# Layout transposes of a hybrid decoder step moved from TensorE to DMA transposes on SyncE's queue

## The chip, the cores and the metric

The kernel runs on the 8 cores of one Trainium2 chip. Each core works on its own two prompt sequences and its own 16 sample sequences, with no traffic between cores. The metric is the device time of the slowest core in microseconds (us). PE is TensorE, ACT is ScalarE, DVE is VectorE, POOL is GpSimd and SP is SyncE; SP computes nothing and only issues DMAs, in the order of its queue.

## The reference

Two layers over prompt sequences of 2048 + 16 tokens and over 8 new tokens of each sample sequence, width 1024. Cut to what matters:

```python
for l in range(DEPTH):
    q, k, v, u = _project(hp, ln1[l], w_in[l])           # rmsnorm, then 1024 -> 512 | 128 | 128 | 512
    a = _prompt_attention(rope(q), rope(k), v, sinks[l]) # 8 heads of 64, window 128, two key/value heads
    pm = _pool_mix(u, ...)                               # causal pooling over 2/4/8/16 tokens, then a small matmul
    hp = hp + concat([a, pm]) @ w_out[l]                 # 1024 x 1024
    hp = hp + _mlp(hp, ln2[l], w_up[l], w_down[l])       # rmsnorm, 1024 -> 4096, relu squared, 4096 -> 1024
y_prompt = _rmsnorm(hp, ln_f)[:, N_META:]
```

The sample sequences go through the same layers with cached keys and values.

## The kernel before, in words

Tokens are cut into 34 tiles of 128 rows: tile 0 holds the meta tokens, tiles 1 to 32 the two prompt sequences, tile 33 the sample tokens. `MACROS` puts them into groups of at most four tiles, 9 groups in each of the two layers, 18 in all. Each group has two phases. `att_phase(q)` runs `att_tile` for each tile: load `h`, normalise it (`norm_T` with gain 0), project (`inproj`), rotate, transpose q and k, pool, scores, exponentials, probabilities times values (`st_pv`), output projection (`oproj`), and normalise again (`norm_T` with gain 1) into `xn2T`. Two tiles are in flight; they use the two sets of buffers (`xhat`, `xnT`, `P`, `PT`, `a`, `mixT`) in turn. `mlp_phase(q)` streams the two large weight matrices in 8 pieces of 1 MB each through two buffers each and alternates blocks of 8 matmuls: `up` (1024 to 512 columns of one piece, for all tiles of the group at once) and `dn` (back to 1024, tile by tile, added into `h` by DVE).

The attention phase of group q + 1 is written beside the MLP phase of group q, and there are 8 slots for `h`, so a tile of group q + 1 can only be loaded when group q - 1 has left its slot through the MLP and the store.

A matmul contracts over the partitions, so everything that becomes an operand must first be turned. Before the change all of this is done on PE through a bank of PSUM and copied out by ACT or DVE: the normalised rows `xhat` into `xnT` or `xn2T` (8 blocks of 128 by 128), the probabilities `P` into `PT` (8 blocks for each of two head groups, `st_pt`) and the attention output `a` into `mixT` (2 blocks for each head group, `st_at`).

The order on every engine is fixed at build time by `list_schedule`. It walks through all operations with a cost for each, lets attention work (`cls` 0) go ahead of MLP work (`cls` 1) when both are ready, and writes the order down; on the chip every engine then works strictly in that order and waits on semaphores. For a DMA it counts:

```python
DMA_BW = {"pool": 330e3, "sp": 200e3, "act": 200e3}
HOP_LAT = 0.35
            issue_end = st + c
            dma_free[e] = max(issue_end, dma_free[e]) + nb / DMA_BW[e]
            fin = dma_free[e] + 2.0
            eng_free[e] = issue_end
```

Of the kernel before, what the change touches and what calls it, by code (L numbers as in the profile page):

```python
# [309 lines left out]
def build_program():  # L310
# [38 lines left out]
    S = Sched()  # L349
# [18 lines left out]
    xn2T_t, _ = sbn("xn2T", 2, [128, 8, 512], BF16)  # L368
# [31 lines left out]
    mix_t, mix_b = sbn("mixT", 2, [128, 8, 128], BF16)  # L400
    kvf_t, kvf_b = sb("kvf", [128, 256])
    st_t, st_b = sbn("stat", 8, [128, 64])
    st_b2 = [Buf("statb%d" % i) for i in range(8)]
# [14 lines left out]
    banks = Banks((4, 5, 6, 7))  # L418
# [21 lines left out]
    def dma(eng, out, in_, reads=(), writes=(), sembuf=None, after=()):  # L440
        return dmas(eng, [(out, in_)], reads=reads, writes=writes, sembuf=sembuf, after=after)

    def act(fn, reads, writes, pw=(), cost=None):
# [16 lines left out]
    first_pe = []  # L460
# [110 lines left out]
    def norm_T(hs, gi, dstT, dstT_b, par, bank):  # L571
# [8 lines left out]
        dve(lambda e: e.scalar_tensor_tensor(out=xh[:], in0=h_t[hs][:], scalar=sT[:, 2:3], in1=g_t[gi][:], op0=ALU.mult, op1=ALU.mult),  # L580
            [h_b[hs], sB, g_b[gi]], [xhb], cost=1.29)
        trps = ps_t[bank].bitcast(BF16)

# [184 lines left out]
    def att_tile(l, ti, hs, par, q, j):  # L768
# [7 lines left out]
        if l or ti not in preloaded:  # L776
            load_x(l, ti, hs)
        while True:
            bk = banks.take(1)
            if bk:  # L780
                break
            yield False
        norm_T(hs, 0, xnT, xnTb, par, bk[0])
        if l == 0 and ti == 0:
            load_rest()
        banks.give(*bk)
        yield True
# [143 lines left out]
        if kind != "sample":  # L931
# [53 lines left out]

            def st_pt(g, bpt):
                ptps = ps_t[bpt].bitcast(BF16)

                def ptr(e):
                    r = None  # L990
                    for h4 in range(4):
                        for hf in range(2):
                            c = (h4 * 2 + hf) * 128
                            r = e.transpose(out=ptps[:, c:c + 128], in_=P[:, g * 4 + h4, hf * 128:(hf + 1) * 128], identity=ident_t[:])  # L994
                    return r
                pe(ptr, [Pg[g], ident_b], [ps_b[bpt]], cost=0.45)
                dst = PT[:, g * 4:(g + 1) * 4, :, :].rearrange("p h f t -> p (h f t)")
                if g == 0:
                    act(lambda e: e.activation(out=dst, in_=ptps[:, :], func=AF.Copy), [ps_b[bpt]], [PTg[g]], cost=1.05)
                else:  # L1000
                    dve(lambda e: e.tensor_copy(out=dst, in_=ptps[:, :]), [ps_b[bpt]], [PTg[g]], cost=0.69)
# [16 lines left out]

            def st_at(g, baT):
                aTps = ps_t[baT].bitcast(BF16)  # L1020

# [27 lines left out]
            yield True  # L1049
            b, = yield from grab(1)  # L1050
            st_pt(0, b)
            banks.give(b)
            st_exp(1, *s1)
# [5 lines left out]
            banks.give(b)  # L1059
            b, = yield from grab(1)  # L1060
            st_pt(1, b)
            banks.give(b)
            yield True
            b, = yield from grab(1)
            st_at(0, b)
            banks.give(b)
            b, = yield from grab(1)
            st_pv(1, b)
            banks.give(b)
            yield True  # L1070
            b, = yield from grab(1)
            st_at(1, b)
            banks.give(b)
            yield True
# [20 lines left out]
        yield True  # L1095
        while True:
            bk = banks.take(1)
            if bk:
                break
            yield False  # L1100
        norm_T(hs, 1, xn2T_t[q % 2][:, :, j * 128:(j + 1) * 128], xn2T_b[q % 2][j], par, bk[0])
        banks.give(*bk)
        yield True
# [195 lines left out]
```

How the kernel before makes its waits and increments, by code:

```python
    def emit(engname, eng):  # L181
        seen = {}
        for idx in order[engname]:
            o = ops[idx]
            waits = {}
            for d in o.deps:
                od = ops[d]
                if _skip_edge(od, o):
                    continue
                s, v = od.tok
                k = id(s)
                if k not in waits or waits[k][1] < v:
                    waits[k] = (s, v)
            for k, (s, v) in waits.items():
                if seen.get(k, 0) >= v:
                    continue
                eng.wait_ge(s, v)
                seen[k] = v
            r = o.fn(eng)
            if o.dma:
                assert len(r) == o.ndma, (len(r), o.ndma)
                for ins in r:
                    ins.then_inc(o.tok[0], 16)
            elif o.tok is not None:
                r.then_inc(o.tok[0], 1)
        if engname == "sp":
            for s, v in finals:
                eng.wait_ge(s, v)
```

## Time and profile before

| | |
|---|---|
| median of 3 runs | 2930.97 us (2930.91 to 2939.81) |
| the profiled execution, device time | 2944.05 us |
| its span on the slowest core (core 1) | 2942.3 us |
| PE busy | 2779.2 us, 94% of the span |
| DVE busy / ACT busy | 1522.4 us / 1535.3 us, 52% each |
| DMA queues, share of 16 engines | 42.5% (POOL's queue), 9.5% (SP's queue) |
| chain that ended last | PE 87%, DMA 9% |

The span is the time from the first to the last instruction of a core. A share of busy time is a mean over stages; the stage from 2262 to 2424 us is one whole period of the program (four tiles through attention, four through the MLP) and is looked at by itself below.

### The profile page before, as it was taken

To read this page: it belongs to the slowest core of one execution; us is meant where nothing else is said; L and a number is where in the kernel's file an instruction comes from. 1 tells how busy PE (TensorE), PEld (TensorE's weight loads), DVE (VectorE), ACT (ScalarE), POOL (GpSimd) and SP (SyncE) were. 2 spreads that over 40 slices of the span, in tenths; PEclk is the share of its full clock that TensorE was granted. 3 is DMA by queue.
4 is the path that set the end of the run, shared out by engine and by line. 5 is a ranking of instruction groups with operands and counts; after the bars stand their busy time and mean duration, and the time that the engine had idled before them with its cause. 6 is when DMAs were issued, how large, how long until landed. Compare 5 with 4: busy or idle time off the path is not lost.

```text
span 2942.3 us, 52160 instructions; the slowest of 8 cores (2901.3 to 2942.3 us)
## 1 busy us (share of the span) xinstructions
PE 2779.2 (94%) x17074; PEld 1446.1 (49%) x17074; DVE 1522.4 (52%) x3188; ACT 1535.3 (52%) x3835; POOL 195.2 (7%) x336
## 2 busy tenths in 40 slices
PE   4789988979899999999999999999899999999997
PEld 2455434445455555545455555454454545555544
DVE  2444534545355555545555555555455555555543
ACT  3545534545355555545454655555554655555543
POOL 1000100100000000000000000000000000000000
PEclk8999989999999999999999999999999999999999
DMA  9599996664756647353625332443325242342446
GB/s 177 88 145 197 178 243 122 146 169 125 195 137 161 189 113 205 101 195 123 229 87 201 114 142 93 154 132 115 117 99 188 87 167 105 117 158 87 160 145 228
DMA packets 115648, 436.41 MB, mean 148 GB/s; under 512 B 18732, under 2 KB 45324, under 8 KB 80216
## 3 DMA queue, kind: packets, MB, share of 16 engines
q0 software_dynamic: 89024, 335.80, 42.5%
q1 hardware_dynamic: 26360, 97.28, 9.5%
q8 instruction: 143, 2.34, 0.3%
q14 instruction: 121, 0.99, 0.1%
HBM read 442.32 MB, written 79.22 MB: 177 GB/s over the span
## 4 chain that ended last, share of the span: by engine, by line
PE 87%; DMA 9%; ACT 1%; issue 1%; DVE 1%; SPq 0%; POOL 0%; ACTq 0%; DVEq 0%; POOLq 0%
PE ps_all L1165 29%; PE ps_all L1147 29%; PE ps_all L801 10%; PE ps_all L1089 8%; DMA s_wup<-w_up 2%; PE ps_all L587 2%; PE ps_all L952 2%; PE ps_all L994 2%; DMA s_wout<-w_out 2%; DMA h_mid<-s_h 1%; DMA s_wdn<-w_dn 1%; DMA s_h<-x_p 1%; PE ps_all L954 1%; PE ps_all L953 1%; DMA s_kc<-ck 1%
## 5 line engine op out<-in xcount | busy, mean ns | idle before, releaser
L1165 PE MATMUL ps_all<-s_wdn,s_aT 128*128 128x512 bf16 x4288 | 1037.5, 382 | 21.6 <-DMA s_wdn<-w_dn 12.5
L1147 PE MATMUL ps_all<-s_xn2T,s_wup 128*128 128x512 bf16 (+2 forms) x4608 | 1023.8, 367 | 19.5 <-DMA s_wup<-w_up 13.2
L1169 DVE TENSOR_TENSOR s_h<-s_h,ps_all 128x512 f32<-128x512 f32 x1072 | 735.1, 686 | 549.1 <-PE ps_all L1165 524.7
L1147 PEld LDWEIGHTS ps_all<-s_xn2T,s_wup 128*128 128x128 bf16 x4608 | 445.1, 98 | 470.1 <-issue 31.0
L1151 ACT ACTIVATE s_relu<-ps_all 128x512 f32<-128x512 f32 (+2 forms) x576 | 326.0, 566 | 626.1 <-PE ps_all L1147 613.8
L1165 PEld LDWEIGHTS ps_all<-s_wdn,s_aT 128*128 128x128 bf16 x4288 | 406.1, 98 | 450.6 <-issue 36.1
L1152 ACT ACTIVATE s_aT<-s_relu 128x512 bf16<-128x512 f32 (+2 forms) x576 | 346.2, 601 | 39.0 <-PE ps_all L1165 5.4
L801 PE MATMUL ps_all<-s_win,s_xnT 128*128 128x512 bf16 (+1 forms) x1632 | 315.0, 350 | 22.5 <-DMA s_win<-w_in 12.6
L976 ACT ACTIVATE s_P<-ps_all,s_stat 128x256 bf16<-128x256 f32 x520 | 239.2, 476 | 91.4 <-DVE s_stat L966 91.3
L1089 PE MATMUL ps_all<-s_wout,s_mixT 128*128 128x512 bf16 x1072 | 249.8, 384 | 2.0 <-ACT s_mixT L1029 1.9
L801 PEld LDWEIGHTS ps_all<-s_win,s_xnT 128*128 128x128 bf16 x1632 | 160.7, 99 | 176.9 <-issue 36.7
L575 ACT ACTIVATE s_xhat<-s_h 128x1024 bf16<-128x1024 f32 x135 | 142.6, 1056 | 145.7 <-DVE s_h L1092 86.0
L960 DVE TENSOR_REDUCE s_stat<-ps_all 128x2 f32<-128x512 f32 x260 | 167.8, 684 | 86.0 <-PE ps_all L954 84.8
L580 DVE SCALAR_TENSOR_TENSOR s_xhat<-s_h,s_stat,s_gbc 128x1024 bf16<-128x1024 f32 x135 | 172.7, 1280 | 64.5 <-ACT s_stat L579 63.9
L436 POOL DMA_DIRECT2D s_wup<-up_bf x128 | 67.8, 530 | 1860.9 <-PE ps_all L1147 1262.8
L820 DVE TENSOR_TENSOR s_ropet<-ps_all,s_rope 128x160 f32<-128x160 f32 x68 | 22.0, 324 | 297.8 <-ACT s_vu L811 294.5
L1092 DVE TENSOR_TENSOR s_h<-s_h,ps_all 128x512 f32<-128x512 f32 x134 | 92.1, 687 | 150.6 <-PE ps_all L1089 148.7
L1089 PEld LDWEIGHTS ps_all<-s_wout,s_mixT 128*128 128x128 bf16 x1072 | 104.8, 99 | 122.2 <-issue 8.9
L587 PE MATMUL ps_all<-s_ident,s_xhat 128*128 128x128 bf16 x1080 | 85.6, 224 | 48.5 <-DVE s_xhat L580 45.1
L587 PEld LDWEIGHTS ps_all<-s_ident,s_xhat 128*128 128x128 bf16 x1080 | 72.5, 100 | 75.9 <-issue 52.5
L976 ACT ACTIVATION_READ_ACCUMULATOR s_P<-ps_all,s_stat 128x1 f32 x520 | 108.7, 209 | 0.0
L952 PE MATMUL ps_all<-s_masks,s_ident 128*128 128x512 bf16 x260 | 98.5, 379 | 2.2 <-ACT s_qT L882 1.3
(130 smaller groups left out, 2016.3 us busy)
## 6 DMA issues: line engine op xcount, KB each, us to landing
s_wup<-up_bf POOLq DMA_DIRECT2D x128, 1024.0 KB, 6.4
s_wdn<-dn_bf POOLq DMA_DIRECT2D x128, 1024.0 KB, 7.2
h_mid<-s_h SPq DMA_DIRECT2D x34, 512.0 KB, 8.1
s_h<-h_mid SPq DMA_DIRECT2D x34, 512.0 KB, 7.9
s_h<-x_p SPq DMA_DIRECT2D x32, 512.0 KB, 9.3
s_wup<-w_up POOLq DMA_DIRECT2D x16, 1024.0 KB, 18.0
s_wdn<-w_dn POOLq DMA_DIRECT2D x16, 1024.0 KB, 19.2
y_p<-s_h SPq DMA_DIRECT2D x32, 512.0 KB, 5.5
```

Source lines behind the costliest of these rows:

```text
L580: dve(lambda e: e.scalar_tensor_tensor(out=xh[:], in0=h_t[hs][:], scalar=sT[:, 2:3], in1=g_t[gi][:], op0=ALU.mult, op1=ALU.mult), [h_b[hs] ...
L587: r = e.transpose(out=trps[:, k * 128:(k + 1) * 128], in_=xh[:, k * 128:(k + 1) * 128], identity=ident_t[:])
L801: r = e.matmul(ps_t[bank][:, 0:c1 - c0], lhsT=xnT[:, k, :], rhs=win_t[:, k, c0:c1], start=(k == 0), stop=(k == 7))
L952: e.matmul(ps_t[bk][:].rearrange("p (s h k) -> p s h k", s=2, h=2), lhsT=ident_t[:], rhs=mask4d, start=True, stop=False)
L960: dve(lambda e, v4=v4, cc0=cc0: e.tensor_reduce(out=sT[:, cc0:cc0 + 2], in_=v4, axis=AX.XY, op=ALU.max), [ps_b[bk]], [], pw=[Ba], cost=0.69)
L976: act(lambda e, v3=v3, hh=hh: e.activation(out=P[:, hh, :].rearrange("p (s k) -> p s k", s=2), in_=v3, func=AF.Exp, bias=sT[:, 16 + hh:17 ...
L1089: r = e.matmul(ps_t[bo][:], lhsT=mix[:, c, :], rhs=wout_t[:, c, hf * 512:(hf + 1) * 512], start=(c == 0), stop=(c == 7))
L1147: r = e.matmul(ps_t[bk][:, 0:n], lhsT=wup_t[s][:, k, fc * 128:(fc + 1) * 128], rhs=x2[:, k, 0:n], start=(k == 0), stop=(k == 7))
L1151: act(lambda e: e.activation(out=r_t[ri][:, 0:n], in_=ps_t[bk][:, 0:n], func=AF.Relu), [ps_b[bk]], [r_b[ri]], cost=0.18 + n / 1210.0)
L1152: act(lambda e: e.activation(out=aT[:, fc, 0:n], in_=r_t[ri][:, 0:n], func=AF.Square), [r_b[ri]], [], pw=[aTb], cost=0.21 + n / 1210.0)
L1165: r = e.matmul(ps_t[db][:], lhsT=aT[:, fc, j * 128:(j + 1) * 128], rhs=wdn_t[s][:, fc, hf * 512:(hf + 1) * 512], start=(fc == 0), stop=(fc ...
L1169: dve(lambda e, hf=hf, db=db: e.tensor_tensor(out=h_t[hs][:, hf * 512:(hf + 1) * 512], in0=h_t[hs][:, hf * 512:(hf + 1) * 512], in1=ps_t[d ...
```

## The change

From the second group on (`q` above 0) the three kinds of turning are done by a DMA transpose that SP issues, straight from SBUF to SBUF, with no PSUM bank, no PE instruction and no copy. The sample tile keeps its own transposes inside its attention, and q and k are still turned on PE. The first group keeps the old way. For `list_schedule` a DMA transpose costs 0.1 us of issue and twice its bytes at 200,000 bytes per us, plus the 2.0 us of every DMA.

```diff
+    mixT_sem = [[Buf("mixT%d_%d" % (i, g)) for g in range(2)] for i in range(2)]
...
+    def dma_T(out, in_, reads, writes, pw=(), sembuf=None):
+        def fn(e):
+            return [e.dma_start_transpose(out=out, in_=in_)]
+        return S.op("sp", fn, reads=reads, writes=writes, pwrites=pw, dma=1, sembuf=sembuf, cost=0.1, nbytes=2 * _nbytes(in_))
...
+        if bank is None:
+            t_op = dma_T(dstT, xh[:], [xhb], [dstT_b], sembuf=dstT_b)
+            if gi == 0:
+                first_pe.append(t_op)
+            return
...
+        by_pe = q == 0
...
-        norm_T(hs, 0, xnT, xnTb, par, bk[0])
+        norm_T(hs, 0, xnT[:], xnTb, par, bk[0] if by_pe else None)
...
             def st_pt(g, bpt):
+                if bpt is None:
+                    dma_T(PT[:, g * 4:(g + 1) * 4, :, :].rearrange("p h f t -> p (h f) t"), P[:, g * 4:(g + 1) * 4, :].rearrange("p h k -> p (h k)"),
+                          [Pg[g]], [PTg[g]], sembuf=PTg[g])
+                    return
...
             def st_at(g, baT):
+                if baT is None:
+                    dma_T(mix[:, g * 2:g * 2 + 2, :], asb[:, g * 256:(g + 1) * 256], [ag[g]], [], pw=[mixb], sembuf=mixT_sem[par][g])
+                    return
...
-            b, = yield from grab(1)
-            st_pt(0, b)
-            banks.give(b)
+            if by_pe:
+                b, = yield from grab(1)
+                st_pt(0, b)
+                banks.give(b)
+            else:
+                st_pt(0, None)
...
-        norm_T(hs, 1, xn2T_t[q % 2][:, :, j * 128:(j + 1) * 128], xn2T_b[q % 2][j], par, bk[0])
-        banks.give(*bk)
+        norm_T(hs, 1, xn2T_t[q % 2][:, :, j * 128:(j + 1) * 128], xn2T_b[q % 2][j], par, bk[0] if by_pe else None)
+        if by_pe:
+            banks.give(*bk)
```

Counted over the program, SP's queue gets 383 DMA transposes: 66 into `xnT`, 65 into `xn2T` and 126 into `PT`, each of 128 by 1024 bf16 values (256 KB), and 126 into `mixT` of 128 by 256 values (64 KB). It had 200 rows of DMAs before.

Since the costs changed, `list_schedule` also writes another order. On SP, over one late period (four tiles of layer 1), the queue held only stores of finished tiles and loads of new ones:

```order
L436 DMA y_p<-s_h 128x1024
L436 DMA s_h<-h_mid 128x1024
L436 DMA y_p<-s_h 128x1024
L436 DMA s_h<-h_mid 128x1024 x2
L436 DMA y_p<-s_h 128x1024 x2
```

In the changed kernel the same queue holds the transposes of the four tiles between them:

```order
L446 DMA_TRANSPOSE s_xn2T<-s_xhat 128x8x128
L446 DMA_TRANSPOSE s_PT<-s_P 128x8x128 x2
L446 DMA_TRANSPOSE s_xnT<-s_xhat 128x8x128
L446 DMA_TRANSPOSE s_mixT<-s_a 128x2x128 x2
L446 DMA_TRANSPOSE s_PT<-s_P 128x8x128
L446 DMA_TRANSPOSE s_xn2T<-s_xhat 128x8x128
L446 DMA_TRANSPOSE s_PT<-s_P 128x8x128
L446 DMA_TRANSPOSE s_mixT<-s_a 128x2x128 x2
L437 DMA y_p<-s_h 128x1024
L446 DMA_TRANSPOSE s_xn2T<-s_xhat 128x8x128
L437 DMA s_h<-h_mid 128x1024
```

What moved: SP's queue, which waited for stores and loads only, now has 24 transposes in a period of four tiles, each of which waits there for the engine that makes its input.

On PE, the turnover from one group to the next. Before, this is the piece from the last tile's output projection (L1089) on, in the period that ends the attention of tiles 27 to 30; L1165 is `dn`, L1147 is `up`, L587 the transposes of the last `xhat`. The first block of `up` that reads this group's `xn2T` is the row behind the last one shown:

```order
L1026 MATMUL ps_all<-s_ident,s_a 128x128 x2
L1165 MATMUL ps_all<-s_wdn,s_aT 128x512 x8
L1089 MATMUL ps_all<-s_wout,s_mixT 128x512 x16
L1147 MATMUL ps_all<-s_xn2T,s_wup 128x512 x8
L1165 MATMUL ps_all<-s_wdn,s_aT 128x512 x8
L1147 MATMUL ps_all<-s_xn2T,s_wup 128x512 x8
L1165 MATMUL ps_all<-s_wdn,s_aT 128x512 x8
L587 MATMUL ps_all<-s_ident,s_xhat 128x128 x8
L1147 MATMUL ps_all<-s_xn2T,s_wup 128x512 x8
L1165 MATMUL ps_all<-s_wdn,s_aT 128x512 x8
```

Now, at the same tile, with L1122 the output projection, L1200 `dn` and L1182 `up`. Here the row of 48 begins with the first block that reads this group's `xn2T`:

```order
L1200 MATMUL ps_all<-s_wdn,s_aT 128x512 x16
L1122 MATMUL ps_all<-s_wout,s_mixT 128x512 x16
L1200 MATMUL ps_all<-s_wdn,s_aT 128x512 x12
L1182 MATMUL ps_all<-s_xn2T,s_wup 128x512 x48
L1200 MATMUL ps_all<-s_wdn,s_aT 128x512 x8
L1182 MATMUL ps_all<-s_xn2T,s_wup 128x512 x8
```

What moved: the eight transposes are gone, and between the last output projection and the first block that needs the last tile's `xn2T` there stand 12 matmuls where there were 48 and the eight transposes.

## Rows read from the trace of the kernel before

**Rows 1.** The page, busy time and share of each engine.

```profile
PE 2779.2 (94%) x17074; PEld 1446.1 (49%) x17074; DVE 1522.4 (52%) x3188; ACT 1535.3 (52%) x3835; POOL 195.2 (7%) x336
```

**Rows 2.** Windows of core 1, engines' busy time; last three: PE clock, DMA share, GB/s.

```profile
0.00:400.00 400.00, 312.36 (x2021) 174.25 (x2022) 172.57 (x388) 186.28 (x500) 34.38 (x47) 0.93 0.90 162
2262.00:2424.00 162.00, 161.92 (x984) 83.28 (x982) 91.97 (x185) 91.44 (x228) 8.45 (x16) 1.00 0.36 131
```

**Rows 3.** Timeline of PE: first and last transposes of one period, and the turnover.

```profile
2262.23 0.61 PE L587 MATMUL ps_all<-s_ident,s_xhat 128*128 128x128 bf16 x8
...
2383.78 3.62 PE L1089 MATMUL ps_all<-s_wout,s_mixT 128*128 128x512 bf16 x16
2387.24 1.89 PE L1147 MATMUL ps_all<-s_xn2T,s_wup 128*128 128x512 bf16 x8
2388.96 1.89 PE L1165 MATMUL ps_all<-s_wdn,s_aT 128*128 128x512 bf16 x8
...
2394.14 0.61 PE L587 MATMUL ps_all<-s_ident,s_xhat 128*128 128x128 bf16 x8
2394.59 1.67 PE L1147 MATMUL ps_all<-s_xn2T,s_wup 128*128 128x512 bf16 x7
...
2423.94 0.61 PE L587 MATMUL ps_all<-s_ident,s_xhat 128*128 128x128 bf16 x8
```

**Rows 4.** Groups of instructions by line: what the change removes, and the norm's chain.

```profile
L587 PE MATMUL ps_all<-s_ident,s_xhat 128*128 128x128 bf16 x1080 | 85.6, 224 | 48.5 <-DVE s_xhat L580 45.1 <-DVE s_stat L963 2.7 <-DVE s_stat L980 0.6
L994 PE MATMUL ps_all<-s_ident,s_P 128*128 128x128 bf16 x1040 | 81.4, 222 | 9.4 <-ACT s_stat L982 9.2 <-ACT s_P L976 0.2
L1026 PE MATMUL ps_all<-s_ident,s_a 128*128 128x128 bf16 x260 | 35.3, 222 | 6.4 <-DVE s_a L1015 2.9 <-DVE s_PT L1001 2.3 <-DVE s_stat L983 0.9
L999 ACT ACTIVATE s_PT<-ps_all 128x1024 bf16<-128x1024 bf16 x65 | 66.5, 1023 | 41.7 <-PE ps_all L994 41.1
L1092 DVE TENSOR_TENSOR s_h<-s_h,ps_all 128x512 f32<-128x512 f32 x134 | 92.1, 687 | 150.6 <-PE ps_all L1089 148.7 <-PE ps_all L587 1.4
L575 ACT ACTIVATE s_xhat<-s_h 128x1024 bf16<-128x1024 f32 x135 | 142.6, 1056 | 145.7 <-DVE s_h L1092 86.0 <-DMA s_h<-x_p 30.2 <-DMA s_h<-h_mid 15.8
L577 ACT ACTIVATE s_stat<-s_stat,s_eps 128x1 f32<-128x1 f32 x135 | 39.3, 292 | 5.7
L579 ACT ACTIVATE s_stat<-s_stat 128x1 f32<-128x1 f32 x135 | 26.8, 199 | 4.0
L580 DVE SCALAR_TENSOR_TENSOR s_xhat<-s_h,s_stat,s_gbc 128x1024 bf16<-128x1024 f32 x135 | 172.7, 1280 | 64.5 <-ACT s_stat L579 63.9 <-ACT s_relu L1151 0.3
```

**Rows 5.** DMA issues: count, KB of each, median us from issue to landing.

```profile
s_wup<-up_bf POOLq DMA_DIRECT2D x128, 1024.0 KB, 6.4
s_h<-h_mid SPq DMA_DIRECT2D x34, 512.0 KB, 7.9
y_p<-s_h SPq DMA_DIRECT2D x32, 512.0 KB, 5.5
s_kc<-ck POOLq DMA_DIRECT2D x8, 128.0 KB, 14.9
s_vc<-cv POOLq DMA_DIRECT2D x8, 128.0 KB, 9.1
s_ident<-ident SPq DMA_DIRECT2D x1, 32.0 KB, 2.0
```

**Rows 6.** DMA view from 1970 to 1985 us: packets; POOL's queue; one lone load.

```profile
DMA packets 1335, 1.01 MB, mean 67 GB/s; under 512 B 1163, under 2 KB 1251, under 8 KB 1251
q0 software_dynamic: 1154, 0.93, 29.1%
s_vc<-cv POOLq DMA_DIRECT2D x1, 128.0 KB, 3.1
```

**Rows 7.** Waits of SP's queue: us in total, times, longest us.

```profile
SPq L197 <- DMA s_wup<-w_up: 129.7, 8, 39.8
SPq L197 <- DMA s_wdn<-w_dn: 81.4, 8, 14.5
```

More of the change, by code:

```diff
@@ L777, in att_tile @@
             load_x(l, ti, hs)
[L778 to L782, printed above, removed]
-        norm_T(hs, 0, xnT, xnTb, par, bk[0])
+        by_pe = q == 0
+        if by_pe:
+            while True:
+                bk = banks.take(1)
+                if bk:
+                    break
+                yield False
+        norm_T(hs, 0, xnT[:], xnTb, par, bk[0] if by_pe else None)
         if l == 0 and ti == 0:
             load_rest()
-        banks.give(*bk)
+        if by_pe:
+            banks.give(*bk)
         yield True
@@ L1049, in att_tile @@
             yield True
-            b, = yield from grab(1)
-            st_pt(0, b)
-            banks.give(b)
+            if by_pe:
+                b, = yield from grab(1)
[3 more added lines that the diff above has]
+                st_pt(0, None)
             st_exp(1, *s1)
@@ L1059, in att_tile @@
             banks.give(b)
-            b, = yield from grab(1)
-            st_pt(1, b)
-            banks.give(b)
-            yield True
-            b, = yield from grab(1)
-            st_at(0, b)
-            banks.give(b)
+            if by_pe:
+                b, = yield from grab(1)
+                st_pt(1, b)
+                banks.give(b)
+            else:
+                st_pt(1, None)
+            yield True
+            if by_pe:
+                b, = yield from grab(1)
+                st_at(0, b)
+                banks.give(b)
+            else:
+                st_at(0, None)
             b, = yield from grab(1)
@@ L1070, in att_tile @@
             yield True
-            b, = yield from grab(1)
-            st_at(1, b)
-            banks.give(b)
+            if by_pe:
+                b, = yield from grab(1)
+                st_at(1, b)
+                banks.give(b)
+            else:
+                st_at(1, None)
             yield True
@@ L1095, in att_tile @@
         yield True
[L1096 to L1100, printed above, removed]
-        norm_T(hs, 1, xn2T_t[q % 2][:, :, j * 128:(j + 1) * 128], xn2T_b[q % 2][j], par, bk[0])
-        banks.give(*bk)
+        if by_pe:
+            while True:
+                bk = banks.take(1)
+                if bk:
+                    break
+                yield False
+        norm_T(hs, 1, xn2T_t[q % 2][:, :, j * 128:(j + 1) * 128], xn2T_b[q % 2][j], par, bk[0] if by_pe else None)
+        if by_pe:
+            banks.give(*bk)
         yield True
```

## The prediction

> **What bounds the kernel now.** I read the page first. PE is busy 94% of the span and DVE and ACT about half of it [rows 1], so PE looks like the bound; but the share is a mean, and the windows say where the rest is. In the first 400 us PE works 312 us, with the DMA engines busy 0.90 of the time. In a late period, 2262 to 2424 us, PE works 161.92 of 162 us at a clock of 1.00 (the level of 2.4 GHz), and the DMA engines are busy 0.36 [rows 2]. So from there on nothing but PE's own list of work sets the time, and 18 groups at 162 us make 2916 of the 2942 us. The timeline of PE shows the second thing that matters. The attention phase of that period runs from the first transposes at 2262.2 to the last ones at 2394.1; the next attention phase starts at 2423.9 [rows 3]. Attention takes 132 of 162 us, and the other 30 us are cover: MLP matmuls that need nothing of it. The change shortens PE's list and lengthens the attention phase. Which of the two ends last decides.
>
> **What it saves.** The program had 1080 transposes of `xhat`, 1040 of `P` and 260 of `a` [rows 4]; without the first group's two tiles, 1048, 1008 and 252 go. Their rows add to 202 us of busy PE, but a duration overlaps the next matmul. From the start of eight transposes to the next matmul is 0.45 us (2394.14 to 2394.59 [rows 3]). That gives (131 + 126) x 0.45 = 116 us, and 126 pairs at about 0.13 us (35.3 us over 260 pieces is 0.14 each, two of them overlapped [rows 4]) 16 us: 132 us, or 7.8 us for each of the 17 changed groups. The copies that go, such as 66.5 us of L999 on ACT [rows 4], lie on engines that are half idle. I cost them at nothing: PE's blocks hide them.
>
> **What a DMA transpose costs.** The trace has none, so I bound one of 256 KB from both sides. Below: 32 KB in 2.0 us with empty DMA engines and 512 KB in 5.5 us [rows 5] give 3.6 us between them, if it runs like a plain copy with rows of 4 KB. Above: `s_kc`, 128 KB in pieces of a few hundred bytes, takes 14.9 us behind weight loads, `s_vc` 9.1 us [rows 5]; alone `s_vc` took 3.1 us [rows 6]. I put the ends at 3.6 and 12 us. Between them I go by pieces: a source of 128 partitions by 8 blocks is 1024 rows of 256 bytes, 64 for each of 16 engines. In a stretch of mostly such packets, 1154 of them took 29.1% of 16 engines over 15 us, 70 us, so 0.06 us each [rows 6]. 64 x 0.06 + 2.0 = 5.9 us; the weight loads keep the engines busy 0.36 of the time [rows 2] and a load lands after 6.4 us [rows 5], so I add 0.6 for sharing: 6.5 us. The small ones into `mixT` have 256 rows and come to about 3.5 us, which 16 matmuls of `dn` at 0.216 us (eight of them from 2388.96 on take 1.73 us) cover.
>
> **Where it is exposed: the turnover.** In the changed order the last tile's output projection is followed by 12 matmuls, then by the first block that needs that tile's `xn2T`. Between them lie now: the addition of the second half on DVE 0.69, square 1.06, its two small steps 0.29 and 0.20, the scaling on DVE 1.28 [rows 4], 3.5 us together; before, the same way took 6.8 us from the end of L1089's slots at 2387.2 to 2394.1 [rows 3], queues included. I take 5.5, plus 6.5 for the transpose. The cover is 12 x 0.216 = 2.6 us. PE stands 5.5 + 6.5 - 2.6 = 9.4 us in each group. Behind the waiting block stands the whole list of PE, since a list is worked off in order; `dn` blocks that could run are behind it too. Before, 48 matmuls (10.4 us) and the eight transposes were the cover, and the wait did not exist.
>
> **Inside the phase.** The list counts 0.1 + 2.6 + 2.0 + 0.35 = 5.1 us for a transpose and puts the consumer (projection, `st_pv`, `oproj`) about there. PE's blocks are longer than counted, so 5.4 us are covered. At 6.5 us each exposed consumer is 1.1 us late. Four tiles have 16 such consumers (`xnT`, two halves of `PT`, the second half of `mixT`); two tiles are in flight, and a stall for one covers the other's, so I count 8: 9 us. SP's queue is in order as well, but its stores and loads wait at the end of a group, where they did before.
>
> **The start.** SP's queue waited 129.7 and 81.4 us in 16 places for weight loads that it had to store again [rows 7], and transposes of the second and third attention phases now stand behind some of them. PE idles there anyway. Bounds 0 and 100 us; I take 25, since most of these waits end before PE's next attention work.
>
> **The sum.** 17 x (9.4 + 9 - 7.8) = 180, plus 25: 205 us on 2944 us, the profiled execution's own time, gives 3149. That execution stood 13 us above the median of 2931, which puts the median at 3136; I round up to 3150, since any unevenness of landing times only adds.
>
> A rule of the Trainium skill speaks for a better price. Advanced Engine Details and Errata, section X-Bar Transpose (TRN2), says that transpose DMAs are as fast as regular ones, at 350 to 400 GB/s. By that 256 KB would need some 0.7 us beyond the 2.0, 2.7 us in all, and by my sum the time would be about 2930, near the second and third rivals below. Another page of the Trainium skill, VectorE: DVE Perf Modes, section The three transpose paths, gives 1309 ns for one 128 by 128 block by DMA; eight blocks in a row would be an estimated 10.5 us beyond 2.0, and the sum about 4060, near the first rival. No row here shows a transpose, so neither page is borne out.
>
> **The rivals.** First, *transposes much slower than 8 us*, because short rows meet weight loads. For it speak 14.9 and 9.1 us of the small pieces under load [rows 5]; against it 3.1 us of the lone one [rows 6]. At 9 us: 17 x (5.5 + 9 - 2.6 + 8 x 3.6 - 7.8) + 25 = 586, 3530 us. At 12 us: 17 x (14.9 + 53 - 7.8) + 25 = 1047, 3990 us. Chance 0.25.
>
> Second, on the other side, *the transposes are hidden and the kernel is faster*. It needs a landing below 3.6 us and DVE and ACT, now relieved, fast enough for the turnover (3.5 instead of 5.5 us). Then the turnover costs 3.5 + 3 - 2.6 = 3.9 us, 3.9 less than is saved, and the time is 2944 - 66 = 2878; with the turnover's wait gone as well, 2944 - 132 = 2812 us. It decides from 10.4 us on, from the last projection to the landed `xn2T` (2.6 of cover and 7.8 saved); below that the group is shorter. For it speaks the 30 us of cover [rows 3], against it that the new list no longer uses this cover there. Chance 0.13.
>
> Third, *a draw*: 3.6 to 5 us. 17 x (5.5 + 4.5 - 2.6 - 7.8) + 25 = 18, 2962; range 2925 to 3040. Chance 0.12, of which 0.04 fall within 0.3% (9 us), about what a measurement of this kernel can tell from no change.
>
> **How the numbers follow.** The forecast (5 to 8 us, 3040 to 3400 us) has 0.50. Slower by over 0.3%: 0.50 + 0.25 + 0.08 = 0.83; faster 0.13; the same 0.04. For the range I leave out about a tenth at either end: below, the hidden case; above, landings over 9.5 us, which is 3600. So 2925 to 3600, and 3040 to 3400 for the forecast alone.
>
> **What would show it.** In the changed kernel's trace: no group of transposes of `xhat`, `P` and `a` beyond the first group's 72 or so; DMA issues of 256 KB with a landing near 6.5 us; a wait of PE for `s_xn2T` of about 9 us, some 16 times, at the first `up` block of a group; shorter waits for `s_PT` and `s_xnT`; periods of about 173 us where 162 were; PE's busy time 130 to 200 us less, and its idle time 350 us more. If the landing is below 4 us, or the wait for `s_xn2T` is absent, the forecast is wrong towards faster; if DMA share goes far above 0.36 and landings pass 9 us, towards slower. If PE's clock falls below 1.00 in a late period, its idle time costs twice, which the sum leaves out.

## The result, and the profile after

The changed kernel takes 1.1183 times as long as before, with an interval of 1.108 to 1.1287: about 3282 us on the 2935 us that the kernel before showed beside it (four runs, 2930.91 to 2955.46). The forecast was 3150 us, 132 us too low, in a range of 2925 to 3600. The median over all four runs is 3455.46 us, because in some executions the cores of one die ran at a granted clock near 0.81; these are left out everywhere here. The profiled execution took 3295.44 us, with a span of 3293.9 us on core 2.

The page of the changed kernel: busy time of the engines, as in [rows 1], then DMA packets, the two large queues (packets, MB, share of 16 engines), and the chain that ended last.

```profile
PE 2721.4 (83%) x14485; PEld 1326.1 (40%) x14766; DVE 1437.6 (44%) x2994; ACT 1373.3 (42%) x3515; POOL 195.2 (6%) x336
DMA packets 423315, 511.84 MB, mean 155 GB/s; under 512 B 326412, under 2 KB 353004, under 8 KB 387896
q0 software_dynamic: 89024, 335.80, 39.3%
q1 hardware_dynamic: 334040, 172.95, 24.8%
PE 59%; DMA 28%; issue 4%; DVE 4%; ACT 3%; SPq 2%; DVEq 0%; ACTq 0%; POOL 0%; POOLq 0%
```

PE has fallen from 94% of the span to 83%, and the DMAs' part of the last chain has risen from 9% to 28%. The list of PE is short by its transposes (14766 weight loads where there were 17074), and 281 records of matmuls are missing in this trace besides, but its busy time is hardly lower. The transposes' queue carries 334040 packets instead of 26360.

The waits of PE in the changed kernel, by line and what ended them: us in total, times, longest us.

```profile
PE ps_all L1029 <- DMA s_PT<-s_P: 177.7, 37, 17.0
PE ps_all L1122 <- DMA s_mixT<-s_a: 113.9, 19, 35.1
PE ps_all L815 <- DMA s_xnT<-s_xhat: 68.8, 18, 10.5
PE ps_all L1182 <- DMA s_xn2T<-s_xhat: 60.7, 10, 9.7
```

These are 421 us in 84 waits. Only 61 us lie at the turnover (L1182); the other 360 are inside the attention phase, at the probabilities times values (L1029), the output projection (L1122) and the projection (L815).

The line that issues the transposes, by what they write: duration of the issue on SP's queue in ns (min/median/max), first and last start. The last row is over all 383.

```profile
L446 SPq DMA_TRANSPOSE s_PT<-s_P x126: 1231/1233/12438, 106.7 to 3149.3; - x126
L446 SPq DMA_TRANSPOSE s_mixT<-s_a x126: 1167/1174/6850, 120.2 to 3162.8; - x126
L446 SPq DMA_TRANSPOSE s_xnT<-s_xhat x66: 1231/1236/17901, 85.2 to 3087.2; - x66
L446 SPq DMA_TRANSPOSE s_xn2T<-s_xhat x65: 1232/1232/14298, 147.2 to 3177.1; - x65
...
DMA to landing us min/median/max: 2.3/4.9/32.4
```

The DMA view gives medians of 5.6 us for `s_PT`, 6.1 for `s_xnT`, 4.2 for `s_xn2T` and 4.0 for the small `s_mixT`. My 6.5 us is a little above all of them. What no median shows is the tail, up to 32.4 us. Nor does it show the tail of the issues: 57 of the 383 held SP's queue for more than 2 us, 259 us of 677 in all.

Each of the 84 waits can be laid beside the transpose that ended it. Those transposes landed after 8.2 us in the median, where all 383 have 4.9, and the 33 of them that landed after more than 10 us carry 265 of the 421 us. Of the 421 us, 341 lie between the end of the issue and the landing, 27 in the issue itself and some 23 behind other work in SP's queue (this last part by pairing transposes and their inputs in order). So the waits come from the tail of the landings, and the queue is a small part.

Windows of both kernels, each from the first store of `h_mid` to the last (nearly all of layer 0) and from there to the end. Columns as in [rows 2]; the first two rows are of before, the others of after, the last two of which are two late groups.

```profile
235.00:1598.00 1363.00, 1305.25 (x7891) 665.91 (x7890) 692.72 (x1473) 689.55 (x1690) 94.84 (x160) 0.98 0.60 161
1598.00:2937.00 1339.00, 1308.91 (x8034) 680.12 (x8031) 731.99 (x1486) 736.70 (x1837) 77.73 (x146) 0.99 0.39 137
```

```profile
238.00:1838.00 1600.00, 1298.22 (x6731) 616.06 (x6863) 663.20 (x1405) 620.75 (x1565) 94.79 (x159) 0.91 0.70 161
1838.00:3289.00 1451.00, 1277.65 (x6856) 624.71 (x6987) 693.37 (x1397) 664.89 (x1694) 78.22 (x147) 0.96 0.53 150
2576.55:2764.26 187.71, 162.03 (x826) 76.47 (x841) 86.77 (x173) 82.38 (x210) 8.45 (x16) 0.94 0.50 139
2764.26:2942.30 178.04, 158.31 (x821) 75.21 (x837) 86.30 (x172) 82.11 (x209) 8.47 (x16) 0.96 0.52 145
```

Layer 0 lost 237 us and layer 1 lost 112, or some 30 us for each of 8 changed groups and 12 for each of 9. I had forecast 10.6 everywhere, from one late period; the late periods came out at 188, 178 and 171 us (the third from 2942.3 to 3113.0 us) for a forecast of 172.6. Layer 0 is also where the DMA engines are busiest, 0.60 before and 0.70 after. And in every row the granted clock is down, 0.91 to 0.96 where it was 0.98 and more.

The turnover that the prediction worked out, in one late group. First PE's timeline (start us, us, operation, idle before it and its releaser, as in [rows 3]), then SP's:

```profile
2879.42 3.61 PE L1122 MATMUL ps_all<-s_wout,s_mixT 128*128 128x512 bf16 x16 [1.80 <-DMA s_mixT<-s_a]
2882.88 2.99 PE L1200 MATMUL ps_all<-s_wdn,s_aT 128*128 128x512 bf16 x12
2892.93 5.14 PE L1182 MATMUL ps_all<-s_xn2T,s_wup 128*128 128x512 bf16 x15 [7.07 <-DMA s_xn2T<-s_xhat]
```

```profile
2887.94 1.24 SPq L446 DMA_TRANSPOSE s_xn2T<-s_xhat  x1
```

All steps are there. From the end of the projection's slots at 2882.88 to the issue are 5.06 us (forecast 5.5), from the issue to the block that waited 4.99 (forecast 6.5), 12 `dn` matmuls cover part of it, and PE stands 7.07 us (forecast 9.4). The last row of PE shows one more thing: this block took 5.14 us, where the 16 matmuls of L1122 took 3.61 (it has 16 weight loads too; one matmul's record is missing). The windows of the same place say why:

```profile
2884.00:2890.00 6.00, 1.79 (x8) 0.47 (x6) 4.54 (x5) 3.29 (x8) 0.53 (x1) 0.94 0.61 203
2890.00:2896.00 6.00, 3.06 (x8) 1.17 (x9) 0.46 (x1) 2.69 (x7) 0.00 (x0) 0.50 0.90 274
2896.00:2902.00 6.00, 5.68 (x26) 2.40 (x26) 3.31 (x3) 5.28 (x12) 0.00 (x0) 1.00 0.72 264
```

While PE stood, the granted clock fell to 0.50, the level of 1.2 GHz, and PE came back on it. So this wait cost 1.5 us more than its 7.07.

### The profile page after: what moved, and what is told of

The parts are those of the page before. It is cut to its first block, busy times and chain, and to the rows that moved or that the text cites. A ratio compares the mean times of both kernels' runs of the same rounds, so it can differ in the third digit from the quotient of the medians.

```text
span 3293.9 us, 47873 instructions; the slowest of 8 cores (3222.7 to 3293.9 us)
## 1 busy us (share of the span) xinstructions
PE 2721.4 (83%) x14485; PEld 1326.1 (40%) x14766; DVE 1437.6 (44%) x2994; ACT 1373.3 (42%) x3515; POOL 195.2 (6%) x336
## 3 DMA queue, kind: packets, MB, share of 16 engines
q1 hardware_dynamic: 334040, 172.95, 24.8%
## 4 chain that ended last, share of the span: by engine, by line
PE 59%; DMA 28%; issue 4%; DVE 4%; ACT 3%; SPq 2%; DVEq 0%; ACTq 0%; POOL 0%; POOLq 0%
PE ps_all L1182 19%; PE ps_all L1200 19%; DMA s_PT<-s_P 10%; PE ps_all L815 8%; PE ps_all L1122 7%; DMA s_xnT<-s_xhat 6%; DMA s_mixT<-s_a 4%; DMA s_xn2T<-s_xhat 2%; DVE s_xhat L586 1%; ACT s_P L990 1%; PE ps_all L966 1%; DMA s_wout<-w_out 1%; SPq L437 1%; DMA h_mid<-s_h 1%; DVE s_stat L974 1%
## 5 line engine op out<-in xcount | busy, mean ns | idle before, releaser
L1182 PE MATMUL ps_all<-s_xn2T,s_wup 128*128 128x512 bf16 (+2 forms) x4527 | 1026.1, 372 | 101.2 <-DMA s_xn2T<-s_xhat 60.7
L1200 PE MATMUL ps_all<-s_wdn,s_aT 128*128 128x512 bf16 x4143 | 1033.5, 386 | 41.3 <-DVE s_h L1204 14.2
L1182 PEld LDWEIGHTS ps_all<-s_xn2T,s_wup 128*128 128x128 bf16 x4608 | 453.6, 100 | 587.4 <-issue 142.8
L1200 PEld LDWEIGHTS ps_all<-s_wdn,s_aT 128*128 128x128 bf16 x4288 | 410.0, 99 | 511.4 <-issue 98.8
L815 PE MATMUL ps_all<-s_win,s_xnT 128*128 128x512 bf16 (+1 forms) x1611 | 327.7, 360 | 82.2 <-DMA s_xnT<-s_xhat 68.8
L1122 PE MATMUL ps_all<-s_wout,s_mixT 128*128 128x512 bf16 x1039 | 264.5, 404 | 117.4 <-DMA s_mixT<-s_a 113.9
L815 PEld LDWEIGHTS ps_all<-s_win,s_xnT 128*128 128x128 bf16 x1632 | 163.1, 101 | 250.0 <-issue 121.0
L1122 PEld LDWEIGHTS ps_all<-s_wout,s_mixT 128*128 128x128 bf16 x1072 | 108.4, 103 | 250.8 <-issue 152.8
L1029 PE MATMUL ps_all<-s_vu,s_PT 128*128 128x64 bf16 x520 | 52.1, 201 | 180.4 <-DMA s_PT<-s_P 177.7
L437 POOL DMA_DIRECT2D s_wup<-up_bf x128 | 67.8, 530 | 1750.8 <-PE ps_all L1182 1414.5
L1033 DVE TENSOR_TENSOR s_a<-ps_all,s_stat 128x256 bf16<-128x256 f32 x130 | 55.0, 423 | 235.4 <-PE ps_all L1030 234.4
L1029 PEld LDWEIGHTS ps_all<-s_vu,s_PT 128*128 128x128 bf16 x520 | 42.5, 103 | 209.1 <-issue 199.3
L437 POOL DMA_DIRECT2D s_wdn<-dn_bf x128 | 67.7, 529 | 779.7 <-PE ps_all L1200 701.5
```

The costliest lines, as they stand in the source:

```text
L437: return [e.dma_start(out=o, in_=i) for (o, i) in pairs]
L815: r = e.matmul(ps_t[bank][:, 0:c1 - c0], lhsT=xnT[:, k, :], rhs=win_t[:, k, c0:c1], start=(k == 0), stop=(k == 7))
L1122: r = e.matmul(ps_t[bo][:], lhsT=mix[:, c, :], rhs=wout_t[:, c, hf * 512:(hf + 1) * 512], start=(c == 0), stop=(c == 7))
L1182: r = e.matmul(ps_t[bk][:, 0:n], lhsT=wup_t[s][:, k, fc * 128:(fc + 1) * 128], rhs=x2[:, k, 0:n], start=(k == 0), stop=(k == 7))
L1200: r = e.matmul(ps_t[db][:], lhsT=aT[:, fc, j * 128:(j + 1) * 128], rhs=wdn_t[s][:, fc, hf * 512:(hf + 1) * 512], start=(fc == 0), stop=(fc ...
```

## The experiments

The theory after the result (A) was that the loss is the transposes' landings, late by some us at many places, longest where they meet weight loads. The rivals were the order and costs of `list_schedule` (B), jams on SP's queue (C), the transpose as an operation against a plain move (D), and PE's clock (E). Ratios are against the kernel before on the same chip.

### One kind of turning at a time

Three kernels keep the DMA way for one kind alone and turn the others on PE. The edit splits `by_pe`; for the first:

```diff
+        pe_n1 = q == 0
+        pe_p = True
+        pe_a = True
...
-            if by_pe:
+            if pe_p:
```

> Only the normalised rows (131 of the 383 transposes: 66 into xnT, 65 into xn2T) go by DMA from the second group on; probabilities and attention outputs are turned on PE as before. PE's list is shorter by 131 x 0.45 = 59 us. Theory A (each transpose's landing is a hop in the chain of attention, so parts cost by their hops, the turnover first): the turnover's wait of about 7 us stays in each of 17 groups (+120), xnT adds some 2 us a group (+35), so 2931 + 120 + 35 - 59 = about 3030, a ratio of 1.03. Theory B (SP's queue is the cost: 1.2 us for each issue and whatever stands ahead in it, so the cost falls much faster than the number of transposes): with a third of the issues the stalls all but go, ratio 0.98 to 1.00.

> Only the probabilities (126 transposes into PT) go by DMA. PE's list is shorter by 126 x 0.45 = 57 us. Theory A: four tiles times one exposed hop of about 2 us a group (+130) less 57: ratio about 1.02 to 1.03. Theory B: as many issues as with the normalised rows, so about the same as that run, 0.98 to 1.00. There is no turnover in it, so that if only the turnover matters it is faster than before by up to 57 us, 0.98.

> Only the attention outputs (126 transposes of 64 KB into mixT) go by DMA. PE's list is shorter by 16 us only. Theory A: 17 groups, some 4 us of exposed waits each, less 16: +50, ratio 1.02. Theory B: an issue of the small ones takes as long as one of the large ones (1.17 against 1.23 us), so it costs as much as each of the other two parts. In the sample groups they stand behind 48 small stores on the queue in both: a wait of 20 to 35 us twice, +50.

Measured: the normalised rows alone 1.0599 (1.0552 to 1.0646), the probabilities alone 1.0384 (1.0297 to 1.047). For the attention output there is one time only, 2972.79 us, some 1.013 times 2935 and without an interval. The three losses add to 0.060 + 0.038 + 0.013 = 0.111, for 0.118 together. So each kind pays by itself, and the loss needs no meeting of the three. For the probabilities alone the waits of PE hold this row:

```profile
PE ps_all L1032 <- DMA s_PT<-s_P: 159.4, 29, 12.0
```

The 126 pieces save 126 x 0.45 = 57 us of PE; 159 - 57 = 102 us, and the span grew by 3033.2 - 2942.3 = 91. For the small pieces, on core 7, the gain of 16 us and the waits of 72 us leave 56 by the same sum, and the span, 2977.3 us, is 35 above that of before.

### The planner's costs and the order

`list_schedule` counted 0.1 us for an issue that holds SP's queue for 1.23. This kernel gives it the measured costs:

```diff
-                    cost=(0.1 if eng == "sp" else 1.0) * len(pairs), ...
+                    cost=(0.4 if eng == "sp" else 1.0) * len(pairs), ...
-        return S.op("sp", fn, ..., dma=1, sembuf=sembuf, cost=0.1, nbytes=2 * _nbytes(in_))
+        return S.op("sp", fn, ..., dma=1, sembuf=sembuf, cost=1.25, nbytes=_nbytes(in_))
```

> The changed kernel with all 383 transposes, but the planner counts what the trace shows: 1.25 us of issue for a transpose and 0.4 us for each other DMA of SP, and half the bytes (landing about 4.9 us with the 2.0). Only the order on the engines changes. Theory A (the chain is too long whatever the order): within 2% of the changed kernel, ratio 1.10 to 1.12. Theory B (the order was written for a queue that issues in 0.1 us, so SP's queue jams): a third or more of the loss comes back, ratio 1.03 to 1.08.

Measured: 1.1155 (1.1098 to 1.1211), no different from after. The order moved and the waits moved with it, `s_mixT` to 59.6 and `s_xnT` to 100.0 us, but their sum stayed near 400. B falls as the planner's costs go; another rule for the order was not tried. This trace has every matmul's record, so I use it below for the account:

```profile
PE 2752.8 (84%) x14766; PEld 1325.2 (40%) x14766; DVE 1437.8 (44%) x2994; ACT 1370.6 (42%) x3515; POOL 195.2 (6%) x336
```

### Moved but not turned, and neither

```diff
-            return [e.dma_start_transpose(out=out, in_=in_)]
+            return [e.dma_start(out=out, in_=in_.rearrange("p (k t) -> p k t", t=128))]
```

> The changed kernel with each of its 383 DMA transposes replaced by a plain DMA copy of the same bytes between the same tiles, so that nothing is turned (the values are not the reference's); the order on all engines and every wait are the same. A plain issue takes 0.33 us on SP's queue where a transpose takes 1.23 us, and moves rows of 256 bytes too. Theory A (any trip through a DMA is a hop of 4 to 5 us in the attention chain): landing about 3.5 us at the median, waits for DMAs on PE go from 422 us to some 250 us, ratio 1.05 to 1.07. Theory B (the transposing itself is the price: issue time and the packets' meeting with weight loads): landing near 2.5 us, ratio 1.00 to 1.03.

The other kernel has the producers (the scaling on DVE, the exponentials, the division) write into `xnT`, `xn2T`, `PT` and `mixT` themselves:

```diff
+        o_ap, o_b = (dstT, dstT_b) if bank is None else (xh[:], xhb)
...
-            t_op = dma_T(dstT, xh[:], [xhb], [dstT_b], sembuf=dstT_b)
```

> Nothing is turned from the second group on: DVE and ACT write their results straight into xnT, xn2T, PT and mixT, with no transposes on PE, no copies and no DMA (the values are not the reference's). It is the floor under every way to turn these tiles. By the price read from the rows before (0.45 us for eight transposes, 132 us in all) PE's list gives 2931 - 132 = 2800, ratio 0.955. If the transposes on PE cost by their busy rows (202 us) or their waits count too, 0.93 to 0.94. If they were hidden, 1.00.

Measured: without any turning 0.95 (0.9482 to 0.9519), a span of 2791.7 us. With plain copies there is one time, 3084.41 us, some 1.049 and without an interval. So the shorter list of PE is worth 5% when nothing takes its place: the forecast was 132 us and 2812, the span fell by 151 to 2792, of which 136 are PE's busy time and 15 its idle time. A trip through the DMA queue in place of it costs about 10 points, and that the trip turns the data another 7. Of the plain copies the issue rows say

```profile
L446 SPq DMA_DIRECT2D s_PT<-s_P x126: 464/465/3407, 109.3 to 2943.4; - x126
...
DMA to landing us min/median/max: 1.8/3.9/26.4
```

A copy holds SP's queue for 0.46 us instead of 1.23 and lands after 3.9 us instead of 4.9. Only 2 of the 383 copies held the queue for over 2 us, where 57 transposes did. The waits of PE for the four are 97.9 + 67.8 + 55.3 + 19.0 = 240 us instead of 421. Even a copy has a tail of 26.4 us, so the tail is not one of transposing (D is a part of the loss, not its root). The page of the kernel without turning has the same list of PE at a higher clock:

```profile
PE 2643.1 (95%) x14766; PEld 1313.3 (47%) x14766; DVE 1429.5 (51%) x2994; ACT 1362.6 (49%) x3515; POOL 195.2 (7%) x336
```

### Without the weight loads

Both kernels, after and before, with the weights loaded for the first three groups only, and 16 conversions of layer 1's weights left out:

```diff
     def convert_next():
         i = n_cvt[0]
-        if i >= len(converts):
+        if i >= 2:
...
     def load_up(gp):
         q, p = divmod(gp, NPIECE)
-        if q >= len(SEQ_M):
+        if q >= 3:
             return
```

> The changed kernel without the weight loads of the MLP from the fourth group on (and without the conversions that feed them), so that the transposes are almost alone on the DMA engines; the MLP works on stale weights (the values are not the reference's). To be set against the kernel before with the same loads left out. Theory of contention (the transposes' packets share the 16 engines with loads of 1 MB): landing falls from 4.9 us to about 3.2 us, tails over 10 us vanish, and the ratio to its partner is 1.05 or less. Theory A without contention: landing stays above 4 us and the ratio stays at 1.09 to 1.12.

> The kernel before with the same weight loads and conversions left out (the values are not the reference's), partner of the run above. PE does not wait for these loads in the kernel before (some 10 us in all from the fourth group on), so 2915 to 2931, ratio 0.995 to 1.00.

Measured: 1.0207 (1.0143 to 1.0272) and 0.9883 (0.9851 to 0.9914). Between the two the change costs 1.0207 / 0.9883 = 1.033, for 1.118 with the loads. For the changed one, the issue rows, its landing and its waits of PE say:

```profile
L446 SPq DMA_TRANSPOSE s_PT<-s_P x126: 1230/1232/11457, 109.4 to 2880.6; - x126
...
DMA to landing us min/median/max: 2.3/3.1/22.1
```

```profile
PE ps_all L1122 <- DMA s_mixT<-s_a: 69.3, 8, 22.0
PE ps_all L1029 <- DMA s_PT<-s_P: 52.8, 9, 14.9
PE ps_all L1182 <- DMA s_xn2T<-s_xhat: 47.7, 9, 13.1
PE ps_all L815 <- DMA s_xnT<-s_xhat: 26.4, 4, 10.3
```

The issue is as long as ever, the landing falls from 4.9 to 3.1 us, and the waits of PE for the four from 421 to 196 us. More than two thirds of the loss go with the weights' stream.

The rest lies in the first three groups, whose weights are still loaded. The last weight load is issued at 665 us in the one kernel and at 562 us in the other. Windows of both, up to the ninth store of `h_mid` and from there to the end, first after, then before:

```profile
0.00:694.30 694.30, 486.31 (x2759) 243.02 (x2759) 255.45 (x592) 250.68 (x675) 50.17 (x72) 0.86 0.84 153
694.30:3009.30 2315.00, 2200.49 (x12009) 1073.64 (x12007) 1181.03 (x2403) 1122.26 (x2840) 5.13 (x8) 0.98 0.25 59
```

```profile
0.00:592.00 592.00, 489.40 (x3160) 262.05 (x3161) 271.01 (x626) 280.20 (x730) 50.19 (x72) 0.94 0.82 158
592.00:2907.00 2315.00, 2280.63 (x13916) 1181.70 (x13914) 1252.34 (x2563) 1259.53 (x3106) 5.14 (x8) 1.00 0.11 32
```

From the ninth store on both take 2315.0 us: without the weights' stream the change costs nothing there. Core by core, four cores agree within 0.3 us and the changed kernel is 7 to 11 us quicker on the other four; with the loads the same stretch is 229 to 281 us longer on every core. So in that stretch the whole loss is the meeting of the transposes with the weights' stream; the conversions and the loads were left out together, and this pair does not part them. Of the 383 transposes 315 start after 720 us, with a median landing of 3.1 us and one landing over 10 us. PE still waits 63 of the 196 us for them there, which the shorter list pays for.

### Small stores, and the conversions

In layer 0 the small stores of the sample tile stood between two transposes: SP's timeline of after had 48 of them from 534.04 to 553.78 us, and PE then stood 23.98 us for `s_mixT`. One kernel stores one of 16 pieces of each:

```diff
-                for s_ in range(16):
+                for s_ in range(1):
```

> The changed kernel, but in the two sample tiles only the first of the 16 pieces of each of three results is stored (45 of 48 small stores of SP's queue left out in each layer, so these outputs are incomplete). In the changed kernel a transpose into mixT stands behind the 48 stores at some 0.42 us each, and PE waited 59 us in two places of that stretch, 24 and 35 us long. Theory of the jammed queue: those two waits go, time falls by 50 to 60 us in that layer and some 20 in the other, ratio 1.09 to 1.10 instead of 1.118. If the transposes there are late for another reason (landing behind weight loads), the ratio stays at 1.11 to 1.12.

Measured: 1.1188 (1.1081 to 1.1296), so C falls for these stores. The 24 us were one wait of 84, and the waits for `s_mixT` were still 93.6 us in all. The part of the waits that lay behind other work in SP's queue fell from some 23 us to 3, and the time did not follow.

Layer 0 also carries the conversions of layer 1's weights into bf16. This kernel leaves 16 of 18 out and reads layer 0's in their place:

```diff
-        if i >= len(converts):
+        if i >= 2:
...
-            dma("pool", flat, up_d[l, p], reads=[up_db[l][p]], ...)
+            dma("pool", flat, up_d[0, p], reads=[up_db[0][p]], ...)
```

> The changed kernel without the 16 conversions that turn layer 1's MLP weights from float32 to bf16 in DRAM while layer 0 runs (two other conversions stay); layer 1's MLP reads layer 0's converted weights, so the values are not the reference's. In the changed kernel layer 0's 8 changed groups (from 238 to 1838 us) are 30 us longer each than before and layer 1's 9 groups (1838 to 3289 us) 12 us. If the conversions' traffic is what makes layer 0 worse, layer 0's end comes 80 to 140 us earlier (at 1700 to 1760 us), with layer 1 unchanged at about 1450 us, ratio 1.07 to 1.09. If it is the loads from float32 and the stores in the second and third group, or the queue, the time hardly moves: 1.105 to 1.12.

Measured: 3223.31 and 3240.46 us, 1.096 and 1.102 times 2940.77, with no interval. Windows of its layers:

```profile
245.70:1764.60 1518.90, 1301.71 (x6864) 615.29 (x6862) 663.55 (x1405) 621.11 (x1564) 81.76 (x143) 0.93 0.64 159
1764.60:3238.70 1474.10, 1290.42 (x6990) 625.25 (x6987) 693.97 (x1397) 665.43 (x1694) 78.28 (x147) 0.95 0.54 148
```

Layer 0 is 81 us shorter than in after, at a DMA share of 0.64 for 0.70, and layer 1 no shorter. It lies between what the theories had expected: the conversions carry a part of the extra loss of layer 0, some 81 of 237 us at most, since the kernel before was not run without them. What makes up the rest of the difference between the layers stays open; the sample tiles, the first groups' loads and the start lie in that stage too.

### PE's clock at the turnover, and the best case for the change

A filler of 28 matmuls of 512 columns behind the last `dn` block ahead of the waiting `up` keeps PE at work there:

```diff
+                for k in range(28):
+                    r = e.matmul(ps_t[UPB[0]][:], lhsT=ident_t[:], rhs=masks_t[:, 0:2, :]..., start=True, stop=True)
...
+            S.op("pe", fill, reads=[ident_b, masks_b], writes=[ps_b[UPB[0]]], cost=0.01, after=[last_dn[0]])
```

> The changed kernel with 28 matmuls of 512 columns, whose result nobody reads, put on PE at each turnover from the third group on, where PE stands 7 us for the last tile's xn2T (16 times 6.0 us of useless work, 97 us of busy time). Theory of the clock (after standing, PE runs its next matmuls at the lower clock, and that costs some 100 us of the loss): the filler costs no time where the wait is as long, PE is warm behind it, and the time is the same or up to 20 us shorter; the granted clock rises from 0.93 to 0.95. Without that effect the time is the same where the wait covers the filler and longer where it doesn't: up to 50 us longer, ratio 1.12 to 1.135.

Measured: 1.126 (1.1186 to 1.1334). PE was busy 2842.2 us, 99.3 of it filler, which leaves 2742.9 for the list that took 2752.8 with the measured costs: the filler gave back some 10 us and cost more than that. It did what it was there for: in the 5 us behind each of the 16 fillers the granted clock is 1.00, where it is 0.69 behind the turnover's wait at 2892.93 us in the changed kernel. But only 10 of the 84 waits lie there, and PE still worked 232 us at a granted clock of 0.50, where it was 250 us in the kernel with measured costs. So waking up at the turnover is no large term by itself.

Last, the version in which nothing should wait: only `xn2T` goes by DMA, for all tiles of a group but the last, which have the rest of the phase as cover (48 transposes). It has the planner's measured costs too, as in the kernel above.

```diff
+        by_pe = True
+        pe_n1 = q == 0 or j is None or j >= len(MACROS[l][SEQ_M[q][1]]) - 1
```

> Only the second normalisation of all but the last tile of each group goes by DMA (49 transposes into xn2T), all else on PE, and the planner counts 1.25 us of issue for a transpose and 0.4 us for other DMAs of SP. These results are needed only when the MLP of the group begins, so the landing has 10 us or more of cover. PE's list is shorter by 49 x 0.45 = 22 us. Theory A: what costs is a landing that is waited for; here none is, so 2931 - 22 + 0 to 10, ratio 0.993 to 1.00. If the longer hold of xhat or the DMA traffic itself costs, ratio 1.01.

Measured: 1.0069 (1.0028 to 1.0109), a miss. PE has no wait for a transpose among its ten largest. The 48 x 0.45 = 22 us that its list is shorter do not show. The waits of L598 for `s_xhat`, 37.9 us, are not the reason, as before had 45.1 us of them (L587, [rows 4]). Set beside the same cores of before, the kernel falls behind by 28 us in the mean between the first and the seventh store of `h_mid` (up to some 590 us, the stage where the loss without weight loads also lay), and gains only 3 from there on. What costs the 28 us there, and whether it is the transposes or the planner's other order, is not shown.

## Why the prediction came out as it did

The direction, the range of the time (3040 to 3400 us) and the kind of cost, PE standing for landings, held; the case's landings of 5 to 8 us are met by two kinds of transposes in the median and missed by the other two. The amount was 132 us short. The account goes from the spans of before (2942.3, PE busy 2779.2, so idle 163.1), of the kernel with measured costs (3278.2, busy 2752.8, idle 525.4) and of the one without turning (busy 2643.1 on the same list of 14766):

| | forecast | measured |
|---|---|---|
| shorter list of PE | -132 | 2643.1 - 2779.2 = -136 |
| PE standing | 17 x (9.4 + 9) + 25 = +338 | 525.4 - 163.1 = +362 |
| the same list taking longer, mostly by a lower granted clock | not in the sum | 2752.8 - 2643.1 = +110 |
| sum | +205 (rounded up to 3150) | +336 |

**What it saves.** Right: 132 us against 136 of PE's busy time, from 0.45 us per eight transposes. The kernel without turning gained 15 us more, in idle time.

**What a DMA transpose costs.** 6.5 us against medians of 5.6 and 6.1 for two kinds, 4.2 for the third, and 4.99 in the turnover shown. The working behind it was wrong in two terms that partly cancelled. The 0.06 us for a short packet was twice too much: the queue's added time, (0.248 x 3293.9 - 0.095 x 2942.3) x 16 = 8598 us over 307680 more packets, is 0.028 each. And the issue itself holds the queue for 1.23 us, of which I had nothing. For `s_PT` the landing alone was 3.1 us in the median where I had 5.9, and the weight loads added 2.5 where I had 0.6 for sharing.

The first rule of the Trainium skill that I had weighed, Advanced Engine Details and Errata, section X-Bar Transpose (TRN2), by which transposes are as fast as regular DMAs, is not borne out by these runs: a plain copy of the same tiles landed after 3.9 us and held the queue for 0.46, a transpose 4.9 and 1.23. By that rule my sum gave 2930 us. The other figure of the Trainium skill, VectorE: DVE Perf Modes, section The three transpose paths, 1309 ns for one block of 128 by 128, does not add up over eight blocks in one DMA, as my estimate of 10.5 us had it: all eight landed in 3.1 us, the median of `s_PT` without weight loads. No run here moved one block alone.

**The turnover.** Right in its parts, too dear in its sum: 7.07 us for 9.4 in the group shown, and 60.7 us in 10 waits where I had 160 in 17. In the group shown PE had just stood 1.80 us for `s_mixT` as well; for the groups without this wait I did not trace where it went.

**Inside the phase.** This step failed in size. I had 17 x 9 = 153 us, from one landing of 6.5 for all and 1.1 us at each of 8 consumers. It measured 177.7 + 113.9 + 68.8 = 360 us in 74 waits, 4.9 each. The term that was mis-sized is the landing under load, put at one median with 0.6 us for sharing: the waits come from the tail, as the pairing above shows. At 5.4 us of cover a median landing of 5.6 costs nearly nothing and one of 32 costs 27. That the standing as a whole, 338 for 362, looks better than its parts is luck: 207 us too little here stand against 99 too much at the turnover and the 25 of the start, and PE's other waits shrank, such as those for `s_xhat`, 45.1 us before and 16.5 after, which the sum left out.

**The start.** I took 25 us for SP's waits for weight stores. What happened is larger and other: all of layer 0 lost 237 us, twice layer 1. The step that failed is to read one late period with a DMA share of 0.36 [rows 2] for 17 groups, though the page's own stage before 1598 us had 0.60.

**The clock.** The term that the sum left out, and the largest part of the 132 us. The prediction named it in its last lines only, as a doubling of the idle time. It cost 110 us on 362 us of added standing, 0.3 us for each, not one. Six kernels have the same list of 14766 matmuls and all their records (us; the last column is PE's busy time in the stretches where the granted clock is 0.50):

| | idle | busy | busy at 0.50 |
|---|---|---|---|
| no turning | 148.6 | 2643.1 | 69 |
| no weight loads | 322.5 | 2686.8 | 140 |
| plain copies | 384.6 | 2698.3 | 151 |
| no conversions | 497.7 | 2741.0 | 232 |
| measured costs | 525.4 | 2752.8 | 250 |
| few small stores | 556.7 | 2756.5 | 256 |

The more PE stands, the longer the same list takes. In the turnover shown above the weight loads of `up` follow each other every 0.43 us at 0.50, twice the 0.216 us of a matmul at 1.00, so half of the last column is what the lower clock cost: 35 us without turning and 125 with the measured costs, a difference of 90 of the 110 us. The other 20 are open.

**The rivals.** The first rival's sum at 9 us comes to 584, not 586, and its 3530 us to 3528, which changes nothing. Transposes slower than 8 us did not come in the median; as a tail, up to 32.4 us, they did, and a rival put as "a few much slower" would have been nearer than "all slower". The hidden case and the draw fail on the same tail, and on the landing of 4.9 us. Where no weights were under way and the median landing was 3.1 us, a draw is what came: 2315.0 us with and without the change, where the prediction's sum at 3.1 us, 5.5 + 3.1 - 2.6 - 7.8 = -1.8 us for each of 15 groups, gives 27 us less. So with the landing alone on the DMA engines the sum comes out within 27 us, and what it lacked was the landing beside the stream. The queue's order and the costs in the planner made no difference.

## What to carry to other kernels

An operation taken off the bounding engine saves what its list is shorter, and this was foretold within 4 us of busy time (19 of the span); its replacement is priced by the tail of its latency at every consumer, so ask for the cover at each of them and read the tail of DMAs that already share those engines, stage by stage. PE's standing is not the whole price either: here each us of it took 0.3 us more, most of it through the lower clock. The same change cost 12% beside a stream of weights and nothing where that stream was off, so ask first what else uses the DMA engines at that time. Small pieces on a DMA queue next to a stream of weights are best tried where a consumer has tens of us of cover, and even there 48 of them brought nothing.

## What the runs showed of the hardware that I had not expected

- A DMA transpose held SP's queue for 1.23 us, and 1.17 for a quarter of the data; a plain DMA of the same tile 0.46. In the median the issue hardly depends on the size. 57 of 383 such issues took over 2 us, up to 17.9; of the plain ones 2 did, up to 3.4.
- The transposes added 307680 packets to their queue, about 1066 for each 256 KB (counting four small ones as one large), at 0.028 us of one DMA engine each; the plain copies added 113392. Yet eight blocks landed in 3.1 us when no weights were under way.
- With weight loads the median landing was 4.9 us and 61 of 383 landed after more than 10 us. From 720 us on in the kernel without them it was 3.1 us, and 1 of 315 did.
- The granted clock fell to 0.50 during one wait of 7 us in a list that had run at 1.00, and the block behind it took 5.14 us instead of 3.61.
